# A decoder step on one core: the last block as straight code with its end by tiles and column halves, the head tokens' parts side by side, and the keys of a head turned together

## The chip, the core and the metric

The kernel runs on one core of a Trainium2 chip. The core has a matrix engine (TensorE, PE in the profile; its weight loads are shown as PEld), a vector engine (VectorE, DVE), a scalar engine (ScalarE, ACT), a general engine (GpSimd, POOL), and an engine that here issues nearly all transfers (SyncE, SP). They work from a shared on-chip memory (SBUF); TensorE writes into accumulation banks (PSUM), eight banks of 512 columns in 128 partitions. Each engine runs its own instruction list, and the lists meet at semaphores. The metric is the device time of one execution in microseconds.

## The reference

One step of a decoder trunk with one layer. 2048 prompt tokens, led by 16 meta tokens, and 8 sample sequences of 4 tokens go through the same weights (D_MODEL 1024, four recurrent heads of 128, D_FF 2816):

```python
def trunk_layer(x, pool_prev, pool_start, S0, conv_prev, lead, n1, w_in, w_pool, pool_scale, lb, g_norm,
                w_out, n2, w_a, w_b, conv_w, conv_b, w_down):
    h = rmsnorm(x, n1)
    z = h @ w_in
    y_pool, pool_new = pool_mix(z[..., :D_POOL], pool_prev, pool_start, w_pool, pool_scale)
    y_rec, S_new = hgrn2_mix(z[..., D_POOL:], S0, lb, g_norm, lead)
    x = x + jnp.concatenate([y_pool, y_rec], axis=-1) @ w_out
    y_ffn, conv_new = conv_ffn(rmsnorm(x, n2), conv_prev, w_a, w_b, conv_w, conv_b, w_down)
    return x + y_ffn, pool_new, S_new, conv_new
```

`hgrn2_mix` is a gated linear attention with a matrix state per head: in each window of tokens the output is masked scores times v, plus q (with its decay) times the state, and the state becomes its decayed self plus the window's decayed keys times v. `conv_ffn` is gelu(conv(h @ w_a)) * (h @ w_b) @ w_down with a causal convolution over three rows. A final RMSNorm gives the outputs y; the last 15 pooling inputs, the states and the last 2 rows of h @ w_a are outputs too (the histories).

## The kernel before

**Blocks.** The prompt is done in four blocks of 512 tokens (`BLOCKS`, `TILES` = 4 tiles of 128). The 16 meta and 32 sample tokens are the "head" tokens, 48 rows (`HEAD`), and go with block 0 only (`hd` = 1 in the code). Each engine's list has `body(0, 1)` as straight code and then a hardware loop, `Fori(1, BLOCKS)`, with `body(b, 0)` for blocks 1 to 3. After the loop stand the turning of the histories (L1203, L1206), their copies on ScalarE (L1667, L1671) and the last stores.

**Three products for one.** Every operand of a large product is split into a high part in fp32r and a low part, what the high part leaves. `three` (L580 to L582) makes a product of high by high, low by high and high by low, all into one bank. In block 0 the weights come raw from HBM, POOL splits them (L552 the high, L556 the low part), SP stores the split units (1 MB each, 96 of them) to HBM, and blocks 1 to 3 load them from there into four slots; a slot is loaded again when TensorE has counted its unit in `unit_done`.

**Order of a block.** The products with w_in by features (forget gates, q, u, gate) and by tokens (v); attention; W_out by tokens; residual and norm; the up products, in an inner loop; and the down products. The down products run over two column halves n, and in each over 22 units of the inner dimension (`pair`, `ktile`), for each unit over the four tiles, in block 0 also the head tokens as a fifth tile with 48 stationary columns. ScalarE casts a unit's activations to the high part (L1573), DVE makes the low part (L2274). Behind some pairs of the second half stand the norm rows of the next block, `row_transposes` (L627), whose rows `x_next` are loaded and squared during the first half. In block 3 they are computed too, from block 0's rows, and nothing uses them. After a half, DVE adds the result tile by tile to x (`half_residual`, L2197, the head tokens' piece L2199). After the second half come the squares (ScalarE, L1217), the root, and the final scaling of whole tiles (DVE, L2313); SP stores y of a block during the next block's products, and of block 3 after the loop (L503), followed by states, pooling rows and convolution rows (L529 to L533).

**Attention** runs over 16 items, four heads times four windows. For item i TensorE turns the decayed keys of the *next* item (`kd_transposed`, L830) into bank 5, ScalarE copies them to SBUF (`kd_tokens`, L1417), and `outputs` makes the masked scores by v (L842), q by the state (L846) and the keys by v (L849), which DVE adds to the state (L2137). L849 waits for the next item's copy, so that it may write its bank.

## Time and profile before

| | |
|---|---|
| runs | 2557.63, 2551.93 and 2554.62 us, median 2554.62 |
| the execution in the profile | 2552.1 us, of which the span is 2550.3 |
| mean granted clock of TensorE | 0.993 |
| TensorE | 2478.0 us busy, 13263 matmuls |
| VectorE, ScalarE, GpSimd | 1187.0, 726.6 and 407.7 us busy |
| transfers | 489.03 MB, mean 192 GB/s |

Times are microseconds from the start of the span. The end of a matmul is modelled, and matmuls overlap, so their pace is read from start to start. An instruction's row gives its start, its length, engine and line, the operation, output and input, and in brackets the idle time of the engine ahead of it with what ended it.

### The profile page before, as it was taken

How to read it: one execution, taken by the hardware profiler on the slowest of the kernel's cores; microseconds unless marked ns; L12 is line 12 of the kernel's file. 1: busy time of each engine (PE TensorE's matmuls, PEld its weight loads, DVE VectorE, ACT ScalarE, POOL GpSimd, SP SyncE). 2: the span in 40 equal slices, each digit the busy share in tenths (PEclk: the TensorE clock that was granted, in tenths of full speed). 3: DMA queues.
4: the chain of work that ended last, by engine and by line, in shares of the span. 5: the costliest groups of instructions: out<-in, count | busy, mean ns of one | idle time of the engine just before them, and what ended most of it. 6: DMA issues, size and time to landing. Idle time of an engine off the chain costs nothing.

```text
span 2550.3 us, 36515 instructions
## 1 busy us (share of the span) xinstructions
PE 2478.0 (97%) x13263; PEld 2100.9 (82%) x13263; DVE 1187.0 (47%) x2307; ACT 726.6 (28%) x1467; POOL 407.7 (16%) x311
## 2 busy tenths in 40 slices
PE   7988999999999999999999999999999999999997
PEld 7878799998778888888887888888887887888886
DVE  6777474333348754222245874222246684222234
ACT  4324132222224332111233332111233342211133
POOL 2235255555540300000000110000000020000000
PEclk9989999999999999999999999999999999999999
DMA  7732467676767224555656424555656523555653
GB/s 246 255 117 75 148 235 262 249 252 244 274 247 263 103 103 178 184 195 184 236 194 238 164 83 154 197 192 186 234 198 214 201 99 132 189 190 188 231 202 133
DMA packets 145350, 489.03 MB, mean 192 GB/s; under 512 B 8881, under 2 KB 79778, under 8 KB 96025
## 3 DMA queue, kind: packets, MB, share of 16 engines
q1 hardware_dynamic: 136747, 482.58, 52.8%
q10 hardware_dynamic: 8472, 4.75, 0.6%
q8 instruction: 77, 1.26, 0.2%
q14 instruction: 54, 0.44, 0.1%
HBM read 375.45 MB, written 112.02 MB: 191 GB/s over the span
## 4 chain that ended last, share of the span: by engine, by line
PE 91%; DVE 3%; issue 2%; DMA 2%; ACT 1%; POOL 1%; SPq 0%; DVEq 0%; ACTq 0%
PE ps L580 23%; PE ps L582 23%; PE ps L581 23%; PE ps L646 12%; PE ps L817 3%; PE ps L627 1%; PE ps L842 1%; DMA w_both<-w_split 1%; PE ps L849 1%; PE ps L611 1%; POOL w_both L556 0%; DVE arena L2115 0%; PE ps L814 0%; PE ps L906 0%; DMA w_raw<-in_w_in 0%
## 5 line engine op out<-in xcount | busy, mean ns | idle before, releaser
L580 PE MATMUL ps<-h_hi,w_both 128*128 128x512 f32 (+1 forms) x1536 | 586.6, 382 | 2.7 <-issue 2.7
L582 PE MATMUL ps<-h_lo,w_both 128*128 128x512 f32 (+1 forms) x1536 | 583.1, 380 | 0.0
L581 PE MATMUL ps<-h_hi,w_both 128*128 128x512 f32 (+1 forms) x1536 | 579.5, 377 | 0.0
L582 PEld LDWEIGHTS ps<-h_lo,w_both 128*128 128x128 f32 x1536 | 288.7, 188 | 59.7
L581 PEld LDWEIGHTS ps<-h_hi,w_both 128*128 128x128 f32 x1536 | 288.6, 188 | 58.8
L580 PEld LDWEIGHTS ps<-h_hi,w_both 128*128 128x128 f32 x1536 | 288.3, 188 | 58.3 <-issue 3.6
L580 PE MATMUL ps<-w_both,act_hi 128*128 128x512 f32 (+1 forms) x748 | 297.4, 398 | 1.8 <-DVE x_tok L2197 1.8
L582 PE MATMUL ps<-w_both,act_hi 128*128 128x512 f32 (+1 forms) x748 | 296.1, 396 | 0.0
L581 PE MATMUL ps<-w_both,act_lo 128*128 128x512 f32 (+1 forms) x748 | 295.5, 395 | 0.0
L2274 DVE TENSOR_TENSOR act_lo<-arena,act_hi 128x512 fp32r<-128x512 f32 (+1 forms) x176 | 137.5, 783 | 329.9 <-ACT act_hi L1573 329.4
L646 PE MATMUL ps<-h_hi,w_both 128*128 128x304 f32 (+1 forms) x1664 | 285.3, 294 | 2.7 <-ACT arena L1379 1.7
L389 POOL TENSOR_TENSOR arena<-arena 128x256 f32<-128x256 f32 x63 | 45.0, 715 | 1304.1 <-DVE arena L2081 1301.9
L2234 DVE SCALAR_TENSOR_TENSOR arena<-arena,vec 128x512 f32<-128x512 f32 x88 | 68.4, 777 | 396.1 <-ACT arena L1499 395.3
L646 PEld LDWEIGHTS ps<-h_hi,w_both 128*128 128x128 f32 x1664 | 237.1, 190 | 3.9 <-ACT arena L1379 2.6
L556 POOL TENSOR_TENSOR w_both<-w_raw,w_both 128x1024 fp32r<-128x1024 f32 x86 | 211.6, 2461 | 7.2
L1573 ACT CAST act_hi<-arena 128x512 fp32r<-128x512 f32 (+3 forms) x176 | 110.5, 630 | 349.2 <-PE ps L582 349.2
L646 PE MATMUL ps<-h_lo,w_both 128*128 128x304 f32 x832 | 174.8, 291 | 0.0
L580 PEld LDWEIGHTS ps<-w_both,act_hi 128*128 128x128 f32 (+1 forms) x748 | 138.3, 185 | 37.4 <-DVE x_tok L2197 2.2
L582 PEld LDWEIGHTS ps<-w_both,act_hi 128*128 128x128 f32 (+1 forms) x748 | 137.9, 184 | 36.3 <-issue 0.2
L581 PEld LDWEIGHTS ps<-w_both,act_lo 128*128 128x128 f32 (+1 forms) x748 | 138.0, 185 | 35.4 <-issue 0.2
L1498 ACT COPY arena<-ps 128x512 f32<-128x512 f32 x66 | 38.7, 586 | 447.5 <-PE ps L582 447.5
L580 PE MATMUL ps<-w_both,h_hi 128*128 128x512 f32 (+1 forms) x408 | 163.6, 401 | 2.1 <-DMA w_both<-w_split 2.1
(254 smaller groups left out, 3323.3 us busy)
## 6 DMA issues: line engine op xcount, KB each, us to landing
w_both<-w_split SPq DMA_DIRECT2D x288, 1024.0 KB, 4.8
w_split<-w_both SPq DMA_DIRECT2D x96, 1024.0 KB, 6.3
w_raw<-in_w_down SPq DMA_DIRECT2D x24, 512.0 KB, 4.3
w_raw<-in_w_a SPq DMA_DIRECT2D x22, 512.0 KB, 4.3
w_raw<-in_w_b SPq DMA_DIRECT2D x22, 512.0 KB, 4.3
w_raw<-in_w_in SPq DMA_DIRECT2D x20, 512.0 KB, 5.5
x_tok<-in_x_prompt SPq DMA_DIRECT2D x16, 512.0 KB, 6.9
arena<-in_x_prompt SPq DMA_DIRECT2D x16, 512.0 KB, 6.8
```

The source lines that it names most:

```text
L389: engine.tensor_tensor(o[:, :, 0:half], bb, gg[:, :, 0:half], ALU.subtract)
L556: nc.gpsimd.tensor_tensor(w_lo[:, s, :], w_raw[:, s, 0, :], w_hi[:, s, :].bitcast(F32), ALU.subtract).then_inc(w_ready, 1)
L580: nc.tensor.matmul(out, lhs[0], rhs[0], start=first, stop=False)
L581: nc.tensor.matmul(out, lhs[1], rhs[0], start=False, stop=False)
L582: return nc.tensor.matmul(out, lhs[0], rhs[1], start=False, stop=last)
L611: last = nc.tensor.matmul(out, w[0][:, k, :], h_lo[:, k, cols], start=False, stop=k == KD - 1)
L646: last = nc.tensor.matmul(out, lhs[:, k, :], rhs[:, k, cols], start=(k, n) == (0, 0), stop=(k, n) == (KD - 1, 2))
L817: last = nc.tensor.matmul(out, m, m, start=True, stop=True)
L1498: nc.scalar.copy(a_ext[:, r, 2:2 + BLOCK], ps[:, r, :])
L1573: nc.scalar.copy(act_hi[:, kk, lo:WIDE], acts[:, bass.ds(2 * i + kk, 1), lo:WIDE].rearrange("p a b -> p (a b)")).then_inc(act_hi_ready, 1)
L2234: own.mark(v.scalar_tensor_tensor(out=cv, in0=ae[:, 1:1 + BLOCK], scalar=w1, in1=cv, op0=ALU.mult, op1=ALU.add))
L2274: v.tensor_tensor(act_lo[:, kk, lo:WIDE], acts[:, bass.ds(2 * i + kk, 1), lo:WIDE].rearrange("p a b -> p (a b)"), act_hi[:, kk, lo:WIDE].b ...
```

## The change

Four things are changed.

1. The loop runs over blocks 1 and 2; block 3 is straight code on each engine (`first(b)` and `final(b)` tell the blocks apart).
2. In block 3 the next block's rows are not loaded, squared, normed and turned. The histories are turned in the second half of down, after pairs 2 and 6. The last two units of the second half go tile by tile (six matmuls for a tile) behind one wait for both units' low parts. The first column half of x is squared and multiplied by the final norm's vector during the second half; behind the last products, roots are taken for two tiles at a time, ScalarE scales front halves and DVE back halves, and y is stored in eight half-column stores behind the other outputs.
3. In block 0 the head tokens' low and high parts lie side by side in one operand of 112 columns (low in 0 to 47, high from 64 on). W_out and down do two matmuls in place of three for them: both by the weights' high part, both by the low part. The result lies in two row groups, which DVE adds one after the other. (The product of low by low is computed along with it.) The v products stay as they were.
4. In attention the four windows' keys of a head are turned together at the head's end, copied in two pieces, and L849 waits at a head's first window only.

```diff
+            def head_product(bank, both, w, first, last):
+                nc.tensor.matmul(ps[0:SIDE + HEAD, bank, :], both, w[0], start=first, stop=False)
+                return nc.tensor.matmul(ps[0:SIDE + HEAD, bank, :], both, w[1], start=False, stop=last)
+            def head_rows_product(bank, k, kk, w):
+                return head_product(bank, h_side[:, k, 0:SIDE + HEAD], [v[:, kk, :] for v in w], k == 0, k == KD - 1)
...
-                def kd_transposed(i):
-                    h, w, n = i // TILES, i % TILES, 16 * b + i
-                    if w == 0:
-                        pe.wait_ge(kd_ready, 4 * b + h + 1)
-                        pe.wait_ge(qe_ready, 4 * b + h + 1)
-                    if not (isinstance(n, int) and n < 1):
-                        pe.wait_ge(kdt_ready, n)
-                    if not (isinstance(n, int) and n < 2):
-                        pe.wait_ge(s_ready, n - 1)
-                    nc.tensor.transpose(ps[:, 5, 0:P], kd[:, h % 2, win(w)], ident).then_inc(kdt_done, 1)
+                def kd_transposed(h):
+                    pe.wait_ge(kd_ready, 4 * b + h + 1)
+                    pe.wait_ge(qe_ready, 4 * b + h + 1)
+                    if not (first(b) and h == 0):
+                        pe.wait_ge(s_ready, 16 * b + 4 * h)
+                    for w in range(TILES):
+                        last = nc.tensor.transpose(ps[:, 5, win(w)], kd_at(h, hd)[:, win(w)], ident)
+                    last.then_inc(kdt_done, 1)
...
-                    pe.wait_ge(kdt_ready, n + (2 if i + 1 < HEADS * TILES else 1))
-                    nc.tensor.matmul(ps[:, 5, P:2 * P], kd_tok[:, i % 2, :], v_tok[:, w, hc], start=True,
+                    if w == 0:
+                        pe.wait_ge(kdt_ready, 2 * (4 * b + h + 1))
+                    nc.tensor.matmul(ps[:, 5, 0:P], kd_token(w, hd), v_tok[:, w, hc], start=True,
                                      stop=True).then_inc(su_done, 1)
...
-                    if i + 1 < HEADS * TILES:
-                        kd_transposed(i + 1)
                     outputs(i)
...
+                    if i % TILES == TILES - 1 and i + 1 < HEADS * TILES:
+                        kd_transposed((i + 1) // TILES)
...
+            def histories(part):
+                pe.wait_ge(x2_ready, 8 * (BLOCKS - 1) + 4)
+                if part == 0:
+                    for g in range(HEADS):
+                        last = nc.tensor.transpose(ps[0:POOL_BUF, 4, win(g)], u_hist[:, g, :], ident)
+                    last.then_inc(last_t, 1)
+                else:
+                    pe.wait_ge(last_taken, 2)
+                for f in range(12 * part, min(FT, 12 * part + 12)):
+                    last = nc.tensor.transpose(ps[0:2, 5 + f % 12 // 4, win(f % 4)], conv_hist[:, f, :], ident)
+                last.then_inc(last_t, 1)
+            def last_tiles(b):
+                for kk in range(2):
+                    weights(b, U_DOWN + 22 + kk, 2 + kk, U_DOWN // 4 + 5)
+                pe.wait_ge(act_lo_ready, 2 * FT * (b + 1))
+                for t in range(TILES):
+                    for kk in range(2):
+                        last = three(ps[:, down_bank(1, t, 0), :], (act_hi[:, kk, main(t)], act_lo[:, kk, main(t)]),
+                                     [w[:, 2 + kk, kk * 512:(kk + 1) * 512] for w in (w_hi, w_lo)], False, kk == 1)
+                    last.then_inc(last_tile, 1)
...
+                    if n and final(b):
+                        for i in range(1, 10):
+                            pair(i, i % 4, False)
+                            if i in (2, 6):
+                                histories(i // 6)
+                        last_tiles(b)
+                        continue
...
-            with pe.Fori(1, BLOCKS) as b:
+            with pe.Fori(1, BLOCKS - 1) as b:
                 body(b, 0)
...
+            body(BLOCKS - 1, 0)
```

ScalarE's and DVE's sides of it:

```diff
-                def kd_tokens(i):
-                    n = 16 * b + i
-                    act.wait_ge(kdt_done, n + 1)
-                    if not (isinstance(n, int) and n < 2):
-                        act.wait_ge(su_done, n - 1)
-                    nc.scalar.copy(kd_tok[:, i % 2, :], ps[:, 5, 0:P]).then_inc(kdt_ready, 1)
+                def kd_tokens(h):
+                    act.wait_ge(kdt_done, 4 * b + h + 1)
+                    if not (first(b) and h == 0):
+                        act.wait_ge(su_done, 16 * b + 4 * h)
+                    for half in range(2):
+                        nc.scalar.copy((kd_late[1 - hd] if half else kd_tok)[:, :, :],
+                                       ps[:, 5, 2 * half * P:2 * (half + 1) * P].rearrange("p (a b) -> p a b", a=2)
+                                       ).then_inc(kdt_ready, 1)
...
+            def head_part(c, bank, side, ready=None):
+                x = x_tok[0:HEAD, TILES, c]
+                last = v.tensor_tensor(x, x, ps[side:side + HEAD, bank, :], ALU.add)
+                if side:
+                    own.mark(last)
+                else:
+                    last.then_inc(ready, 1)
...
+                if hd:
+                    head_part(c, to(TILES), SIDE)
                 for t in range(TILES):
                     v.tensor_tensor(x_tok[:, t, c], x_tok[:, t, c], ps[:, to(t), :], ALU.add).then_inc(ready, 1)
                     if hd and t == 0:
-                        v.tensor_tensor(x_tok[0:HEAD, TILES, c], x_tok[0:HEAD, TILES, c],
-                                        ps[0:HEAD, to(TILES), :], ALU.add).then_inc(hready, 1)
+                        own.settle()
+                        head_part(c, to(TILES), 0, hready)
...
+                add(0)
+                add(1)
+                variance(0)
+                add(2)
+                newton(0)
+                back(0)
+                add(3)
+                back(1)
+                variance(1)
+                newton(1)
+                back(2)
+                back(3)
```

The last twelve lines are DVE's order behind the last products: `add` adds a tile's second column half to x, `variance` and `newton` make the roots of two tiles, `back` scales a back half. ScalarE squares back halves 0 and 1, makes the first guess for tiles 0 and 1, squares half 2, scales front half 0, squares half 3, makes the second guess, and scales the other front halves.

## Rows read from the trace of the kernel before

**Rows 1.** Summary page: span, busy time of each engine, chain's shares, instruction transfers.

```profile
span 2550.3 us, 36515 instructions
...
PE 2478.0 (97%) x13263; PEld 2100.9 (82%) x13263; DVE 1187.0 (47%) x2307; ACT 726.6 (28%) x1467; POOL 407.7 (16%) x311
...
q8 instruction: 77, 1.26, 0.2%
...
PE 91%; DVE 3%; issue 2%; DMA 2%; ACT 1%; POOL 1%; SPq 0%; DVEq 0%; ACTq 0%
```

**Rows 2.** Waits of TensorE, whole run: us in total, times, longest.

```profile
PE ps L849 <- ACT arena L1417: 9.9, 14, 1.5
PE ps L830 <- DVE state L2137: 9.1, 9, 1.7
...
PE ps L580 <- issue: 2.7, 2, 1.4
```

**Rows 3.** Timeline of TensorE, two units of block 0's down products.

```profile
676.00 0.39 PE L580 MATMUL ps<-w_both,act_hi 128*48 128x512 f32 x1
...
680.19 0.39 PE L580 MATMUL ps<-w_both,act_hi 128*128 128x512 f32 x1
```

**Rows 4.** Waits of TensorE, 602 to 764 us, block 0's down products.

```profile
PE ps L580 <- DVE x_tok L2197: 1.8, 1, 1.8
```

**Rows 5.** Timeline, turn of column halves in block 0's down products.

```profile
682.87 0.67 DVE L2199 TENSOR_TENSOR x_tok<-x_tok,ps 48x512 f32<-48x512 f32 x1
...
684.19 0.50 PE L580 MATMUL ps<-w_both,act_hi 128*128 128x512 f32 x1 [1.77 <-DVE x_tok L2197]
```

**Rows 6.** Timeline of POOL: one subtraction of a weight split in block 0.

```profile
671.89 2.77 POOL L556 TENSOR_TENSOR w_both<-w_raw,w_both 128x1024 fp32r<-128x1024 f32 x1
```

**Rows 7.** Windows: length, PE, PEld, DVE, ACT, POOL, clock, DMA share, GB/s.

```profile
686.00:688.00 2.00, 2.00 (x6) 1.55 (x5) 0.98 (x3) 0.66 (x1) 1.45 (x2) 0.50 0.60 255
```

**Rows 8.** Timeline of DVE, head tokens' add of W_out in block 0.

```profile
303.59 0.68 DVE L1804 TENSOR_TENSOR x_tok<-x_tok,ps 48x512 f32<-48x512 f32 x1 [10.68 <-PE ps L582]
```

**Rows 9.** Waits of TensorE, 264 to 345 us, W_out and first up, block 0.

```profile
PE ps L605 <- POOL w_both L556: 2.2, 2, 1.9
```

**Rows 10.** Waits of TensorE, 825 to 935 us, block 1's attention.

```profile
PE ps L830 <- DVE state L2137: 1.7, 1, 1.7
PE ps L849 <- ACT arena L1417: 1.2, 3, 0.9
PE ps L830 <- ACT arena L1417: 0.4, 1, 0.4
```

**Rows 11.** Timeline of block 1's attention, the longest wait for a key copy.

```profile
906.06 0.27 ACT L1417 COPY arena<-ps 128x128 f32<-128x128 f32 x1
...
906.37 0.49 PE L849 MATMUL ps<-arena 128*128 128x128 f32 x2 [0.92 <-ACT arena L1417]
```

**Rows 12.** Waits of TensorE, 165 to 262 us, block 0's attention.

```profile
PE ps L849 <- ACT arena L1417: 6.2, 5, 1.5
```

**Rows 13.** Timeline of block 3's down, one group of the unused norm's transposes.

```profile
2502.61 1.03 PE L627 MATMUL ps<-tab,arena 128*128 128x128 f32 x8
...
2503.72 0.39 PE L581 MATMUL ps<-w_both,act_lo 128*128 128x512 f32 x1
```

**Rows 14.** Timeline of block 3's down, start of the last two units.

```profile
2526.67 0.39 PE L580 MATMUL ps<-w_both,act_hi 128*128 128x512 f32 x1
...
2527.76 0.69 DVE L2274 TENSOR_TENSOR act_lo<-arena,act_hi 128x512 fp32r<-128x512 f32 x1 [2.13 <-ACT act_hi L1573]
```

**Rows 15.** Timeline behind the last matmul.

```profile
2532.47 2.48 DVE L2197 TENSOR_TENSOR x_tok<-x_tok,ps 128x512 f32<-128x512 f32 x4 [4.01 <-PE ps L582]
...
2536.86 1.06 ACT L1217 ACTIVATE arena<-x_tok 128x1024 f32<-128x1024 f32 x1
...
2539.52 4.87 DVE L2313 SCALAR_TENSOR_TENSOR x_tok<-x_tok,norms,arena 128x1024 f32<-128x1024 f32 x4
```

**Rows 16.** Windows, stores of y at the end, columns as in rows 7.

```profile
2542.00:2546.00 4.00, 0.00 (x0) 0.00 (x0) 2.40 (x3) 0.41 (x2) 0.00 (x0) 0.50 1.01 408
```

More of the change, by code:

```diff
@@ L112, in shape_tables, with first, final @@
     return t
+def first(b):
+    return isinstance(b, int) and b == 0
+def final(b):
+    return isinstance(b, int) and b == BLOCKS - 1
 class Order:
@@ L454, in body @@
                     unit(b, s, U_Q + s, U_Q // 4, raw(s, KD), w_in_t[:, :, 512 + s * P:512 + (s + 1) * P])
-                if not isinstance(b, int):
+                if not first(b):
                     store_y(b - 1)
@@ L488, in body @@
                                 sp.wait_ge(act_ready, FT * (b + 1))
-                            for t in range(TILES):
+                            for t in () if final(b) else range(TILES):
                                 sp.dma_start(x_next[:, t, :],
@@ L559, in ahead @@
             def ahead(b):
-                for h in (1, 2, 3) if isinstance(b, int) else (2, 3):
+                for h in (1, 2, 3) if first(b) else (2, 3):
                     if h == 1:
@@ L571, in _ @@
                 units(j)
-            with pool.Fori(1, BLOCKS) as b:
+            with pool.Fori(1, BLOCKS - 1) as b:
                 ahead(b)
+            ahead(BLOCKS - 1)
         @block.tensor
@@ L1128, in ktile @@
                                 pe.wait_ge(x2_ready, 8 * b + 2)
-                            cols = main(t) if t < TILES else slice(0, HEAD)
-                            out = ps[:, down_bank(n, t, hd), :] if t < TILES else ps[0:HEAD, down_bank(n, t, hd), :]
-                            last = three(out, (act_hi[:, kk, cols], act_lo[:, kk, cols]),
-                                         [w[:, slot, wk * 512:(wk + 1) * 512] for w in (w_hi, w_lo)], first, fin)
+                            ws = [w[:, slot, wk * 512:(wk + 1) * 512] for w in (w_hi, w_lo)]
+                            if t == TILES:
+                                last = head_product(down_bank(n, t, hd), act_wide[:, kk, 0:SIDE + HEAD], ws, first, fin)
+                                continue
+                            last = three(ps[:, down_bank(n, t, hd), :], (act_hi[:, kk, main(t)], act_lo[:, kk, main(t)]),
+                                         ws, first, fin)
                         return last
@@ L1255, in decays @@
                         g = g_t[:, h, HEAD:WIDE]
-                        if not (isinstance(b, int) and h == 0):
+                        if not (first(b) and h == 0):
                             act.wait_ge(s_ready, 16 * b if h < 2 else 16 * b + 4 * (h - 1))
@@ L1606, in body @@
                 pair(1, 0, True)
+                if final(b):
+                    last_columns(b, pair)
+                    return
                 root_guess(var[:, :], rstd[:, :], var_ready, 2 * b + 2, guess_ready)
@@ L1663, in _ @@
             body(0, 1)
-            with own.loop(1, BLOCKS, 14) as b:
+            with own.loop(1, BLOCKS - 1, 14) as b:
                 body(b, 0)
-            act.wait_ge(last_t, 1)
-            nc.scalar.copy(last_rows[0:POOL_BUF, :], ps[0:POOL_BUF, 0, :]).then_inc(last_taken, 1)
-            act.wait_ge(last_t, 2)
-            for i in range(6):
-                m = min(4, FT - 4 * i) * P
-                last = nc.scalar.copy(conv_rows[0:2, 4 * i * P:4 * i * P + m], ps[0:2, 1 + i, 0:m])
-            last.then_inc(last_taken, 1)
+            body(BLOCKS - 1, 0)
             act.wait_ge(u_rows_ready, 17)
@@ L2089, in operand @@
                     dve.wait_ge(su_done if i else a_done, n)
+                if first(b) and h and i == LEVELS:
+                    dve.wait_ge(kdt_done, h)
                 dve.wait_ge(dec_exp, 8 * (4 * b + h) + i + 1)
@@ L2285, in down @@
                     pair(0, i)
+                if final(b):
+                    last_columns(b, pair)
+                    return
                 dve.wait_ge(squared, 12 * b + 12)
@@ L2353, in _ @@
             body(0, 1)
-            with own.loop(1, BLOCKS, 122) as b:
+            with own.loop(1, BLOCKS - 1, 122) as b:
                 body(b, 0)
+            body(BLOCKS - 1, 0)
 def kernel(x_prompt, x_sample, state_pool, state_rec, state_conv, meta_tokens, norm1_g, w_in, w_pool, pool_scale,
```

208 lines of the change are left out of this document (159 added, 49 removed).

## The prediction

> **What bounds the kernel now.** I read the summary page first. TensorE is busy for 97% of the span and holds 91% of the chain that ended last; DVE, the next engine, is busy for 47% [rows 1]. So a matmul that disappears is worth its full pitch, and work of another engine counts only where TensorE waits for it or after TensorE's last matmul. Second, the waits of TensorE over the whole run, to see how much idle time there is to win: the large rows are the attention's, 9.9 us for ScalarE's copy of the turned keys (L1417) and 9.1 us for DVE's state (L2137), and 2.7 us are the two returns of the hardware loop [rows 2]. Third, the timelines of the places that the diff touches. The run profiled took 2552.1 us against a span of 2550.3; the sum below is made against 2552.1. The median of the three runs, 2554.62, lies 2.5 above it.
>
> **Head tokens side by side.** In block 0's down products each head product is three matmuls with 48 stationary columns, and they leave at the same pitch as the wide ones: 4.19 us for the 18 starts from 676.00 to 680.19 (three with 48 columns, twelve with 128, three with 48 again), which is 0.233 each [rows 3]. A pitch of the wide matmuls that differed from the narrow ones' would show in that count of 18, so for 112 columns I take 0.233 too. So a product falls from three to two, 0.233 saved. Down has 22 units of the inner dimension times two column halves, 44 products: 10.25 us. W_out has 8 times two, 16 products: 3.73 us. The V products keep three.
>
> What this adds: the result lies in two row groups of a bank, so DVE adds two 48x512 pieces where it added one. At the turn from the first column half of down to the second, TensorE has its only wait of that stage, 1.77 us for DVE's second tile [rows 4, 5]; DVE does a 128x512 and a 48x512 add ahead of it, the latter 0.67 us [rows 5]. The extra add and its settle come ahead of that second tile, so the wait grows by 0.67 to 0.9; I take 0.9. Down: -9.35. It has a cover to lose: block 0's weights are split by POOL, and the subtraction begun at 671.89 took 2.77 us, to 674.66, for a product that starts at 680.19, a lead of 5.5 us [rows 3, 6]. TensorE's unit gets about 0.47 us shorter (two products), so over the three units until POOL's slot is reused the lead falls by about 1.4; 4 us stay. Without that lead the saving would be bounded by POOL.
>
> After the 1.77 us wait the granted clock stands at 0.50 in 686 to 688, the lower level of 1.2 GHz [rows 7]. The wait does not vanish, so I leave that cost (about 1.5 us, an estimate: eight matmuls at some 0.43 instead of 0.23) where it is.
>
> In W_out the saving passes through two other chains: DVE's head add, 0.68 us, now twice [rows 8], and POOL's split of the next weights, for which TensorE waits 2.2 us right behind this stage already [rows 9]. Those splits start when TensorE frees a slot, which comes earlier too, so most of the gain gets through. Bounds: -3.73 (all of it) to 0 (POOL's chain sets the time). I take -3.3, as the slot's release moves with the products. Head tokens: -9.35 - 3.3 = -12.65.
>
> **Keys of a head together.** In block 1 the waits of the attention are 1.7 us on the state, 1.2 on ScalarE's key copies in three places and 0.4 more on them ahead of the transposes, whose bank the copy frees [rows 10]. The largest, 0.92 us at 906.37, is a copy of 0.27 us that started only at 906.06 [rows 11]. With one transposition and two copies for a head, thirteen of sixteen items need nothing from ScalarE: 1.2 + 0.4 = 1.6 us go, and some 0.2 at about four restarts (the row at 906.37 shows 0.49 us for two where a running pair has 0.39), 0.9 together: -2.5. Against it, at three head boundaries two copies of 256 columns must both end before the first key product: from the 0.27 us of 128 columns [rows 11] an estimated 0.4 each, so 0.8 in place of 0.27, of which about 0.2 lies behind outputs that are issued first: +0.35 each, +1.05. I take -1.5 for each of blocks 1 to 3, -4.5; bounds -2.5 (the copies hidden) and +1.5 (the copies late behind ScalarE's other work at each head). The 1.7 us on the state stay: the product with the state waits for the same event if the transpose no longer does.
>
> In block 0 the same copies cost 6.2 us in five waits [rows 12], because ScalarE's exponentials stand ahead of them. Half of it I expect to move to the next thing late (DVE's masking and POOL's exponents of the head): -3.1, with +0.4 for the extra pieces in the pool rows of the head: -2.7, bounds -6 and +1.
>
> **Straight last block.** One of two loop returns goes: 2.7/2 [rows 2], -1.4. The four groups of eight transposes of the unused norm go: from the first of them at 2502.61 to the second matmul behind them at 2503.72 are 1.11 us, less one pitch of 0.23: 0.88 a group [rows 13], 3.5 together. The 26 history transposes that move in from behind the loop cost 0.11 each, by the same row, 2.9, and 0.1 of restarts: +3.0. Net -0.5. They stand where the outputs of the first half have long been added.
>
> **Last two units tile by tile.** The first tile now waits for the low parts of both units. Before, the product began at 2526.67 while DVE's low part of the second unit started at 2527.76 (0.69 us, to 2528.45) [rows 14]. TensorE can start at about 2528.5: +1.9, bounds 1.7 and 3.6, the upper if the clock falls behind it as in [rows 7]. ScalarE and DVE have nothing else queued there that is longer than that, if their front-half work is done by then.
>
> **The end.** DVE starts the last adds at 2532.47, right behind the last matmul's end E, and the span ends at 2550.3, 17.9 us later [rows 1, 15]. In between stand four adds (2.48 us, 0.62 each), four squares of 1024 columns of which the last starts at 2536.86 (1.06 us), the root, and four scalings of 1.22 us from 2539.52 on [rows 15]; the stores follow. After: the tiles come 1.4 us apart (six matmuls of 0.233), so that three of them are added, squared or stored before E. Behind E stand one add (0.62), one half square (1.06/2 and its read, 0.7), the root (1.6, from 2537.92 to 2539.52) and two half scalings (1.2): 4.1 us, and I add 2 for the hand-overs between engines and ScalarE's front halves, an estimate: E+6.1. Six of the eight stores of 256 KB are then left, from E+5.7 on at the 408 GB/s of 2542 to 2546 [rows 16], 0.64 us each: to E+9.6. With 0.8 to close the span, an estimate, it is E+10.4. So 17.9 - 10.4: -7.5; bounds -5 (hand-overs of 4 us) and -9 (none, and the stores at the root's heels).
>
> **Sum.** -12.65 - 2.7 - 4.5 - 1.4 - 0.5 + 1.9 - 7.5 = -27.35: 2552.1 - 27.35 = 2524.75. I say 2525. Own range 2518 to 2531.
>
> **Rivals.** (1) Grouping the keys pays nothing: ScalarE's two copies are late at every head and each boundary gives back what the items save. For it: the 906.06 copy was late behind ScalarE's own work [rows 11], and that work stays. Against: only three boundaries a block are left. 2525 + 4.5 + 2.7 = 2532.
>
> (2) Block 0's down becomes bound by weights: POOL was 2.77 us on half a unit [rows 6], and if a unit's chain of load, split and store is not released by TensorE but runs at its own rate, the 9.35 are lost: 2534. Against it: no wait on POOL is among the waits of down in block 0 [rows 4].
>
> (3) The other side: the straight block pays for its code. Instruction transfers are 77 packets of 1.26 MB in all, 16 KB each [rows 1]. TensorE's straight code of one block is an estimated 18 such packets (about 3,300 matmuls a block by a quarter of 13263, less those in the up loop, two instructions each). If each were waited for like a loop return, 1.35 us, that is +24, and 2549, or 2552 with some on the other engines. Slower by over 0.2% needs 27.35 + 5.1 = 32.45 us, 24 such waits. Against it: block 0 is straight code already, and its waits on issue are only the loop's two [rows 2].
>
> The Trainium skill (Runtime: NRT & Kernel Launch, "Instruction fetch mechanics") says that sequential code is streamed ahead mostly hidden and that a taken branch out of the window forces a fetch before execution goes on. By that rule rival 3 costs nothing and the -1.4 stands; the two 1.3 us gaps at the returns agree.
>
> (4) More is won: the keys' grouping reaches its bounds (-2.5 a block and -6): 2525 - 3.0 - 3.3 = 2518.7, and with an end of -9, 2517.
>
> **Chances.** The forecast 0.5; rival 1 0.2; rival 2 0.07; rival 4 0.15; rival 3 0.08, of which half ends slower. The bound of a readable difference is 0.2%, 5.1 us. Faster 0.92, same 0.04, slower 0.04. The range reaches from rival 4 with a little more from its end (2513) to rival 2 with a low gain at the end (2538).
>
> **What would show it.** Right: L581 on the 128*48 operands gone from down, two instructions with 112 columns at a pitch of 0.23; the 1.77 us wait at the column turn grown to some 2.6; no wait of the key products on ScalarE except at a head's first item; one loop return; an idle of about 1.9 us before the last tiles; and 10.4 us from the last matmul to the end of the span. Wrong: a pitch above 0.23 at 112 columns, issue waits spread over block 3, waits on POOL in block 0's down, or the half-tile stores ending later than E+9.6.

## The result and the profile after

The changed kernel took 2533.69 us (median of 4 runs, 2528.01 to 2536.31) against 2553.27 before: ratio 0.9914, interval 0.9901 to 0.9928, so 19.6 us less. In two later sets of runs the same code stood 25.0 us (ratio 0.9902, 0.9888 to 0.9917) and 23.8 us (0.9909, 0.9892 to 0.9925) below the kernel before. The forecast was 2525 with a range of 2513 to 2538: the direction, the range and most of the terms held, and the gain that was forecast, 27.35 us, was 2 to 8 us too large. The narrower "own range" of 2518 to 2531 holds the two later medians, 2529.80 and 2529.40, and not the first. The number alone would fit rival 1 (2532) and rival 2 (2534) as well; only the stages tell them from the forecast.

The summary page of the changed kernel, to be read against [rows 1]:

```profile
span 2526.2 us, 35716 instructions
...
PE 2460.3 (97%) x13171; PEld 2097.3 (83%) x13171; DVE 1178.4 (47%) x2346; ACT 717.1 (28%) x1435; POOL 409.5 (16%) x311
...
q8 instruction: 74, 1.21, 0.2%
...
PE 91%; DVE 3%; DMA 2%; ACT 1%; issue 1%; POOL 1%; SPq 0%; DVEq 0%; ACTq 0%
```

The span is 24.1 us shorter and TensorE is as full as before. The straight code did not cost more instruction transfers: 74 packets against 77.

Where the 24.1 us lie is read from the starts of the first and the last matmul of each stage in the two traces (a scores product starts attention, and its end is taken as the start of the last window's scores; a product with the activations starts down). "Again" is a second trace of the same code.

| stage | before | changed | difference | again | forecast |
|---|---|---|---|---|---|
| start to the end of block 0's attention | 250.44 | 248.99 | -1.5 | -1.6 | -2.7 |
| block 0, from there to down | 350.89 | 347.51 | -3.4 | -3.0 | -3.3 |
| block 0, down | 162.27 | 155.92 | -6.35 | -6.6 | -9.35 |
| block 1, down's end before it to its down | 462.18 | 460.65 | -1.5 | -1.5 | -1.5 |
| block 2, the same | 463.92 | 462.51 | -1.4 | +0.2 | -1.5 |
| block 3, the same, with the loop's return | 463.97 | 460.74 | -3.2 | -3.3 | -2.9 |
| block 3, down | 126.12 | 127.32 | +1.2 | +1.2 | +1.4 |
| last matmul's start to the end | 18.28 | 10.35 | -7.9 | -7.9 | -7.5 |

(In block 2 of the second trace the granted clock falls to 0.50 for 3.4 us from 1443 us on.) Two rows miss by more than 1 us: block 0's down, and the first, in which two effects of opposite sign are added up (see "The changed kernel again").

The head products in block 0's down, from the timeline of TensorE: start, length, instruction.

```profile
670.74 0.39 PE L613 MATMUL ps<-w_both,act_wide 128*128 128x512 f32 x1
...
670.97 0.39 PE L695 MATMUL ps<-w_both,act_wide 128*112 128x512 f32 x1
...
671.20 0.40 PE L696 MATMUL ps<-w_both,act_wide 128*112 128x512 f32 x1
...
671.44 0.40 PE L611 MATMUL ps<-w_both,act_wide 128*128 128x512 f32 x1
```

Two in place of three [rows 3], 0.23 to 0.24 apart: 112 columns leave at the pitch of 128, as assumed. So the 10.25 us were saved, and something gave part of them back. The waits of TensorE from 596 to 770 us, block 0's down, where before there was one of 1.8 us [rows 4]:

```profile
PE ps L611 <- DVE x_tok L2342: 3.0, 1, 3.0
PE ps L611 <- DVE act_lo L2419: 1.6, 2, 1.1
```

The wait at the turn of the column halves grew by 1.2 us (forecast 0.9), and there are new ones of 1.6 us for DVE's low parts: -10.25 + 1.2 + 1.6 = -7.45, where -6.35 was measured. Of the 1.1 between them some 0.4 are, by an estimate, restarts behind the waits; 0.7 I can't assign.

Attention of block 0, the waits from 165 to 262 us, against [rows 12]:

```profile
PE ps L884 <- DVE arena L2260: 6.5, 5, 2.7
...
PE ps L893 <- ACT arena L1539: 1.5, 1, 1.5
```

The 6.2 us in five waits for ScalarE's key copies are one wait of 1.5, and 6.5 us in five places now go to DVE's last step on the masked scores (L2260): part of the stall went to the next thing late. Part of it is gone: with the waits of attention that are not shown here (4.2 us on DVE's state before, none now) its waits were 12.3 us in 14 places and are 10.1 in 7. In block 1 (820 to 935 us, against [rows 10]) no key copy is waited for:

```profile
PE ps L871 <- DVE state L2276: 1.9, 2, 1.8
PE ps L770 <- DVE arena L2305: 0.5, 1, 0.5
PE ps L884 <- DVE arena L2265: 0.3, 1, 0.3
```

The last units and the end, from the timeline, against [rows 14, 15]:

```profile
2508.49 0.40 PE L613 MATMUL ps<-w_both,act_wide 128*128 128x512 f32 x1
...
2510.41 0.47 PE L611 MATMUL ps<-w_both,act_wide 128*128 128x512 f32 x1 [1.52 <-DVE act_lo L2419]
...
2515.87 0.40 PE L613 MATMUL ps<-w_both,act_wide 128*128 128x512 f32 x1
...
2520.42 1.41 DVE L2495 SCALAR_TENSOR_TENSOR x_tok<-x_tok,norms,arena 128x512 f32<-128x512 f32 x2
...
2522.67 0.64 SPq L563 DMA_DIRECT2D out_y_prompt<-x_tok  x1
```

TensorE stands 1.5 us before the last tiles. With E for the end of the last matmul, 2516.27, the back halves are scaled by 2521.8, which is E+5.6 where the forecast had E+6.1, and the span ends at E+9.9 (forecast E+10.4).

### The profile page after: what moved, and what is told of

Its sections match the earlier page's. It is cut to its first block, busy times and chain, and to the rows that moved or that the text cites. A ratio compares the mean times of both kernels' runs of the same rounds, so it can differ in the third digit from the quotient of the medians.

```text
span 2526.2 us, 35716 instructions
## 1 busy us (share of the span) xinstructions
PE 2460.3 (97%) x13171; PEld 2097.3 (83%) x13171; DVE 1178.4 (47%) x2346; ACT 717.1 (28%) x1435; POOL 409.5 (16%) x311
## 4 chain that ended last, share of the span: by engine, by line
PE 91%; DVE 3%; DMA 2%; ACT 1%; issue 1%; POOL 1%; SPq 0%; DVEq 0%; ACTq 0%
PE ps L611 23%; PE ps L613 23%; PE ps L612 23%; PE ps L677 13%; PE ps L861 3%; PE ps L884 1%; PE ps L658 1%; DVE arena L2254 1%; PE ps L642 1%; DMA w_both<-w_split 1%; PE ps L695 1%; PE ps L696 1%; PE ps L893 1%; POOL w_both L586 0%; PE ps L950 0%
## 5 line engine op out<-in xcount | busy, mean ns | idle before, releaser
L611 PE MATMUL ps<-w_both,act_wide 128*128 128x512 f32 x704 | 280.7, 399 | 6.1 <-DVE act_lo L2419 3.1
L613 PE MATMUL ps<-w_both,act_wide 128*128 128x512 f32 x704 | 278.6, 396 | 0.0
L612 PE MATMUL ps<-w_both,act_lo 128*128 128x512 f32 x704 | 278.2, 395 | 0.0
L2419 DVE TENSOR_TENSOR act_lo<-arena,act_wide 128x512 fp32r<-128x512 f32 x176 | 122.8, 699 | 244.3 <-ACT act_wide L1696 244.1
L1696 ACT CAST act_wide<-arena 128x512 fp32r<-128x512 f32 (+3 forms) x176 | 110.5, 630 | 349.8 <-PE ps L613 249.2
L611 PEld LDWEIGHTS ps<-w_both,act_wide 128*128 128x128 f32 x704 | 132.9, 189 | 39.0 <-DVE x_tok L2342 3.4
L611 PE MATMUL ps<-w_both,h_hi 128*128 128x512 f32 (+1 forms) x392 | 157.4, 401 | 2.1 <-DMA w_both<-w_split 2.1
L613 PEld LDWEIGHTS ps<-w_both,act_wide 128*128 128x128 f32 x704 | 132.6, 188 | 32.0
L612 PEld LDWEIGHTS ps<-w_both,act_lo 128*128 128x128 f32 x704 | 132.8, 189 | 30.4
```

What stands on the lines that cost most here:

```text
L611: nc.tensor.matmul(out, lhs[0], rhs[0], start=first, stop=False)
L612: nc.tensor.matmul(out, lhs[1], rhs[0], start=False, stop=False)
L613: return nc.tensor.matmul(out, lhs[0], rhs[1], start=False, stop=last)
L1696: nc.scalar.copy(act_hi[:, kk, lo:WIDE], acts[:, bass.ds(2 * i + kk, 1), lo:WIDE].rearrange("p a b -> p (a b)")).then_inc(act_hi_ready, 1)
L2419: last = v.tensor_tensor(out[:, kk, cols], acts[:, bass.ds(2 * i + kk, 1), cols].rearrange("p a b -> p (a b)"), act_hi[:, kk, cols].bitcas ...
```

## Experiments

**Each part alone.** Three kernels take over one part of the change each: the head tokens' parts (4 of its lines below), the keys, and the last block.

```diff
+act_wide = sb("act_wide", [P, 2, SIDE + WIDE], F32R)
+h_side = ...  # [P, KD, 2 * SIDE]
+last = head_product(down_bank(n, t, hd), act_wide[:, kk, 0:SIDE + HEAD], ws, first, fin)
+head_part(c, to(TILES), SIDE); own.settle(); head_part(c, to(TILES), 0, hready)
```

> The kernel before with the head tokens' parts side by side and nothing else of the change. First theory (each part keeps its own effect, and the parts add): block 0's W_out 3.4 us shorter, its down products 6.3 us shorter, with the wait at the turn of the column halves near 3 us instead of 1.77 and one or two waits of 0.5 to 1.2 us for the low part made by DVE; in all 9 to 10 us below the kernel before. Second theory (the down products lost their 3 us to something of the other parts, as the memory that the keys and the last block use): the down products 9 to 10 us shorter here, in all 12 to 13 us. On the stage of the sample tokens ahead of attention, which was 4 us longer in the changed kernel's profile: if that is a clock that varies from execution to execution, it may fall here or not, and does not follow the edit; if the changed kernel's code makes it, one of the three part kernels must show it and the others not.

Measured: 2547.06 against 2554.46, -7.4 us (0.997, 0.9958 to 0.9982). In its trace W_out to down is 2.75 us shorter and down 3.95, with a wait of 3.8 at the turn and 1.8 for low parts: the shortfall belongs to this part and the other parts don't make it. The second theory fell. The first was too high, by about 2 us in all; in down, 6.9 us stood at a granted clock of 0.50 here and 3.4 in the kernel before's trace.

```diff
-for i: kd_transposed(i + 1); outputs(i)
+for i: outputs(i); ...; if i % TILES == TILES - 1: kd_transposed((i + 1) // TILES)
```

> The kernel before with the keys of a head turned and copied together, and nothing else. First theory: blocks 1 to 3 each 1.5 us shorter in attention, as in the changed kernel; block 0's attention 3 to 6 us shorter, part of which hangs on the granted clock there; in all 7.5 to 10 us below the kernel before. Second theory (grouping pays nothing by itself; what attention gained came from the clock at its start): blocks 1 to 3 within 0.3 us of before each, and block 0 within 1 us when compared at the same clock; in all 0 to 2 us.

Measured: 2547.75, -6.7 us (0.9971, 0.9962 to 0.998), less than the 7.5 to 10 of the first theory. In its trace block 0's attention is 81.0 us long where it was 85.7, so 4.6 shorter, with 5.5 us of it at a granted clock of 0.50 in place of 8.2. Block 3 is 1.6 us shorter from down to down; blocks 1 and 2 were not shorter in this trace, and the windows of the three blocks' attention at the same place show why (columns as in [rows 7]):

```profile
866.00:868.00 2.00, 2.00 (x6) 1.71 (x7) 1.93 (x5) 0.58 (x3) 0.00 (x0) 0.50 0.00 0
...
1457.00:1459.00 2.00, 2.00 (x7) 1.52 (x6) 2.00 (x5) 0.00 (x0) 0.58 (x1) 0.50 0.00 0
2045.00:2047.00 2.00, 1.93 (x15) 1.66 (x14) 1.93 (x3) 1.32 (x5) 0.00 (x0) 1.00 0.00 0
```

In blocks 1 and 2 the granted clock fell to 0.50, the level of 1.2 GHz, for 3.4 us right behind the wait of 1.8 us on DVE's state, and in block 3, behind the same wait, it did not. One such fall costs about the 1.5 us that a block wins. Grouping pays; the second theory fell.

```diff
-with pe.Fori(1, BLOCKS) as b: body(b, 0)
+with pe.Fori(1, BLOCKS - 1) as b: body(b, 0)
+body(BLOCKS - 1, 0)   # with histories, last_tiles and last_columns
```

> The kernel before with block 3 as straight code and its new end, and nothing else. First theory: one return of the loop less (1.6 us), the down products of block 3 1.2 us longer (1.7 us idle ahead of the last two units against 0.5 us fewer transposes), 10.2 to 10.4 us from the last matmul to the end of the span instead of 17.9: in all 8 to 8.5 us below the kernel before. Second theory (straight code pays at its pages, and the other parts hide it): waits on issue spread over block 3, and in all less than 5 us.

Measured: 2543.42, -11.0 us (0.996, 0.9947 to 0.9974; the -8 to -8.5 of the first theory is inside). In the trace: loop's return -1.7, down +1.2, end 10.37 us from the last matmul's start, one wait on issue of 1.4 in the whole run. The stages named give -8.4; the rest of the -11.0 I can't assign, though its five runs had mean clocks of 0.992 to 0.994, where most of the 16 runs beside them had 0.990 to 0.992. The three parts sum to -7.4 - 6.7 - 11.0 = -25.1; the whole change gave -25.0 and -23.8 in the later sets. The parts add within their intervals, each of which is 2 to 3.5 us wide to either side; that they meet to a tenth is luck.

**The changed kernel again**, unaltered.

> The changed kernel once more, unaltered, as the measure for the other three on one chip. First theory (between the profile of before, 2552.1, and that of the changed kernel, 2528.0, lies 27 us of work less 4 us of clock, and the clock is drawn anew in each execution): the stage of the sample tokens, from 100 to 182 us, again has two to four falls of the granted clock to 0.5 for 6.8 us or longer, at other places than in the first profile; the stages behind it as in the first profile within 0.4 us where the clock stands at 1.00; median 19 to 25 us below the kernel before. Second theory (the changed code itself fixes the falls): the same falls at the same places, and the start of attention again at 168.9.

Measured: 2529.80 against 2554.84. The clock fell at other places than in the first profile, so the second theory fell. TensorE reached block 0's attention at 165.10 us here and at 168.91 in the first trace, since the clock fell more often in the sample tokens' stage there; attention's last scores product started at 248.88 and 248.99. So attention itself was 3.7 us longer here. Its window in three traces, the kernel with the head part alone, the changed kernel and "again" (columns as in [rows 7], the clock is the third number from the end):

```profile
168.89:252.84 83.95, 72.27 (x574) 69.38 (x573) 64.88 (x96) 34.35 (x101) 44.97 (x49) 0.98 0.18 64
...
168.91:248.99 80.08, 70.61 (x574) 69.06 (x574) 64.38 (x94) 33.62 (x93) 44.96 (x49) 0.98 0.19 67
...
165.10:248.88 83.78, 74.32 (x574) 72.82 (x574) 64.56 (x94) 33.60 (x93) 44.96 (x49) 0.93 0.18 64
```

| trace | keys | attention starts | its length | of it at 0.50 | length less half of that |
|---|---|---|---|---|---|
| before | one by one | 164.76 | 85.68 | 8.2 | 81.6 |
| head part alone | one by one | 168.89 | 83.95 | 3.8 | 82.1 |
| keys alone | of a head together | 170.89 | 81.04 | 5.5 | 78.3 |
| changed | of a head together | 168.91 | 80.08 | 3.8 | 78.2 |
| again | of a head together | 165.10 | 83.78 | 11.7 | 77.9 |
| last two units in another order (below) | of a head together | 170.15 | 83.33 | 11.0 | 77.8 |

The waits of attention are the same in the changed kernel and in "again" (6.5 us in five places on L2260 in both), so these don't absorb a late start: the stage is as long as its work and its waits, plus half of the time that the clock stands at 0.50. The last column, an estimate on that footing, is 77.8 to 78.3 us in nine traces with the keys together and 81.5 to 82.1 in the four with single keys. The two traces that start within 0.02 us of each other at a mean clock of 0.98, the head part alone and the changed kernel, differ by 3.9 us. So in block 0 the keys gave 3.3 to 3.9 us. Between the profiles of before and changed, attention starts 4.15 us later, with the clock at 0.50 for 23.5 us ahead of it in place of 12.3, and its own clock gives 2.2 us back; this net loss of 2.0 us hid part of the keys' gain in the table's first row, -1.5. The first theory's clock, 4 us in its estimate, was there, and half of it came back inside attention. (In block 0's down, too, the near agreement of the table, -6.35 and -6.6, has two parts: "again" waits 2.8 us for low parts where the first trace waits 1.6, and its clock does not fall there.)

Whether the change itself makes the clock fall more often ahead of attention stays open. Attention starts at 164.4 to 167.2 us in the three traces without the head part and the keys (before, the last block alone, and the one with two subtractions below) and at 165.1 to 170.9 in ten that have one of them or both, so the head part alone (168.89) and the keys alone (170.89) both show the later start, which the expectation for the head part wanted of one part only. The mean clocks of whole runs don't decide it: they are 0.9915 in the 47 runs of the kernel before that stand beside the experiments and 0.9916 in the 12 of the changed kernel, but they count the end, where TensorE is idle and the clock stands at 0.50 for 12 us in the profile of before and for 5 to 7 in those of the changed kernel.

**The order of the last two units.**

```diff
-for t in range(TILES): for kk in range(2): ...          # behind one wait for both low parts
+for t, kk in ((0,0), (1,0), (0,1), (1,1), (2,0), (2,1), (3,0), (3,1)): ...   # a wait for each kk
```

> The changed kernel with the last two units in another order: the first unit's products for tiles 0 and 1, then the second unit's for both, then tiles 2 and 3 with both units each; only the second unit's products wait for its low part. First theory (the 1.7 us idle ahead of the last tiles is the wait for the second unit's low part, and 1.4 us of products fit into it): the idle falls to 0.3 us or less, tile 0 is ready 0.7 us later against the last matmul and nothing waits for it there, since the root of tiles 0 and 1 waits for tile 1: 1.3 to 1.5 us shorter than the changed kernel. Second theory (something behind the last matmul sets the end, as the stores or ScalarE's chain): the end moves back with the idle by less than 0.5 us.

Measured: 2529.05 against 2554.46 (0.9904, 0.9891 to 0.9918). No wait stands in block 3's down from 2400 us on; the stage is 125.89 us where the changed kernel's is 127.32 (-1.4), and the end is 10.51 where it was 10.35. In the trace the first theory held; no runs of the changed kernel stand in the same set, so the times don't show it.

**The order of DVE's adds at the turn.**

```diff
-head rows 64 to 111; tile 0; head rows 0 to 47; tile 1; tile 2; tile 3
+tile 0; tile 1; head rows 64 to 111; tile 2; head rows 0 to 47; tile 3
```

(The rows from 64 on are the high part's and are added first; the expectation has the two names the other way round.)

> The changed kernel with another order of DVE's adds at the two ends of block 0's down halves: tiles 0 and 1 first, then the head tokens' low part, tile 2, the head tokens' high part, tile 3. First theory (the wait of 2.97 us at the turn is DVE's queue, two adds of the head tokens ahead of tile 1, of which the change brought one): the wait falls by 1.3 us to 1.6 or 1.7; where the clock no longer falls behind it, 1.6 us more are won; median 1 to 3 us below the changed kernel. Second theory (the wait is for DVE's low part, late behind POOL, and not for the adds): the wait falls by less than 0.5 us.

Measured: 2528.45 against 2529.80 for the changed kernel, not to be told apart. The waits of its down in block 0:

```profile
PE ps L611 <- DVE act_lo L2420: 4.2, 4, 2.5
PE ps L611 <- DVE x_tok L2346: 1.5, 1, 1.5
```

The turn's wait fell from 3.0 to 1.5, as the first theory has it, and in this execution the waits for low parts grew to 4.2 us, so that down took 157.71, with one fall of the clock as in the changed kernel. The largest of them in the timeline, with the engine after the length:

```profile
679.48 0.22 DVE L2420 TENSOR_TENSOR act_wide<-arena,act_wide 128x64 fp32r<-128x64 f32 x1
679.52 2.40 POOL L586 TENSOR_TENSOR w_both<-w_raw,w_both 128x1024 fp32r<-128x1024 f32 x1
...
679.63 2.84 DVE L2420 TENSOR_TENSOR act_lo<-arena,act_wide 128x512 fp32r<-128x512 f32 x1
...
682.61 0.47 PE L611 MATMUL ps<-w_both,act_wide 128*128 128x512 f32 x1 [2.45 <-DVE act_lo L2420]
```

DVE's 128x512 subtraction took 2.84 us, where the changed kernel's 176 of them take 0.70 on average; it began 0.1 us behind POOL's subtraction and ended 0.6 behind its end. The kernel before has the same delay, and its trace could have shown it ahead of the prediction:

```profile
620.89 2.40 POOL L556 TENSOR_TENSOR w_both<-w_raw,w_both 128x1024 fp32r<-128x1024 f32 x1
620.96 2.93 DVE L2274 TENSOR_TENSOR act_lo<-arena,act_hi 128x560 fp32r<-128x560 f32 x1 [3.48 <-ACT act_hi L1573]
```

There 18 of the 44 subtractions of block 0's down took over 1 us, all of them while POOL worked, and TensorE waited for none [rows 4]. The nine that met no work of POOL took 0.74 us at most.

**What makes the waits for low parts.** The changed part brings DVE a second instruction for each unit, and it makes TensorE's unit shorter. Two kernels take these apart. The first has both new orders, of the last units and of DVE's adds, and the shorter unit without the instruction (from the third unit on the head tokens' new low part is left out):

```diff
-((act_wide, slice(0, SIDE)), (act_lo, slice(HEAD, WIDE)))[1 - hd:]
+((act_wide, ...), (act_lo, ...))[0 if hd and n == 0 and isinstance(i, int) else 1:]
```

> The kernel with both new orders, without DVE's 128x64 subtraction in block 0's down products except for the first two units (so the head tokens are multiplied with a stale low part from the third unit on; the number and form of the matmuls stays). First theory (the new waits of 0.4 to 2.5 us for DVE's low parts come from the second subtraction that the side-by-side operand needs): those waits vanish from 600 to 765 us, or one of under 0.5 us stays, and the down products are 1.5 to 2 us shorter than with both orders. Second theory (they come from TensorE itself, whose unit is 0.47 us shorter, so that a subtraction that is held up while POOL's runs is no longer covered): the waits stay at two or three, 1.2 us or more together.

Measured: 2525.80 against 2552.20 (0.9903, 0.9879 to 0.9927). Its waits in block 0's down:

```profile
PE ps L611 <- DVE act_lo L2420: 3.0, 2, 2.3
PE ps L611 <- DVE x_tok L2346: 1.3, 1, 1.3
```

The second has the instruction in the kernel before:

```diff
-v.tensor_tensor(act_lo[:, kk, 0:WIDE], ...)
+v.tensor_tensor(act_lo[:, kk, 0:64], ...); v.tensor_tensor(act_lo[:, kk, 64:WIDE], ...)
```

> The kernel before with DVE's 128x560 subtraction of block 0's down products cut into a 128x64 and a 128x496 one, and nothing else: the extra instruction with TensorE's old pace. First theory (the second subtraction makes the waits): two or three waits for the low part of 0.4 to 2 us in the down products, 1 to 3 us slower there. Second theory (TensorE's shorter unit makes them): no wait for the low part, the stage within 0.3 us of before at the same clock.

Measured: 2554.84 against 2552.20 (1.0011, 1.0 to 1.0022). Its waits there:

```profile
PE ps L580 <- DVE x_tok L2197: 2.8, 1, 2.8
PE ps L580 <- DVE act_lo L2275: 0.3, 1, 0.3
```

Without the instruction the waits for low parts stay (3.0 us), and with it at the old pace they don't come (0.3; the kernel with the keys alone, at the old pace without it, shows one of 0.4). The first theory fell, and the second holds for the waits: TensorE's shorter unit no longer covers a subtraction that is held up beside POOL's. Its other half, a stage within 0.3 us, did not: down took 163.84 us against 162.27, of which 1.0 is the wait at the turn (2.8 against 1.8 [rows 4]). DVE's last two subtractions ahead of it took 2.25 us, beside POOL's, where the single one took 1.26; how much of this is the extra instruction and how much the moment at which POOL worked, one trace does not show.

**Both orders together.**

> The changed kernel with both new orders, of DVE's adds at the turn and of the last two units' products. First theory: the two gains add, 2.5 to 4 us below the changed kernel in the stages (1.3 at the turn, 1.4 ahead of the last tiles), which the medians of five runs show only roughly, since the clock moves single runs by 3 us either way. Second theory: one of the two is taken back at the end by the stores: less than 1.5 us.

Measured: 2529.61 against 2529.80, with single runs from 2524.09 to 2532.61: not decided. So both were run once more side by side.

> The kernel with both new orders again, beside the changed kernel on one chip, because the clock moved single runs by more than the 2.8 us that the stages show (1.3 to 1.5 at the turn, 1.5 ahead of the last tiles). First theory: its median lies 2 to 4 us below the changed kernel's. Second theory (the waits that the turn frees come back as waits for DVE's low parts, as the kernel with the turn alone showed): 0 to 1.5 us.

> The changed kernel again, unaltered, as the measure for the kernel with both orders on one chip: 24 to 26 us below the kernel before by either theory, with two to four falls of the granted clock in the stage of the sample tokens.

Measured: 2525.74 (2523.11 to 2526.86; 0.989, 0.9874 to 0.9907) against 2529.40 (2529.17 to 2532.34) for the changed kernel: -3.7 us, and no run of the one reaches the other's. In the traces block 0's down is 153.88 us against 156.01 and block 3's 125.92 against 127.34: 2.1 + 1.4. Not all of it is the orders': in block 0's down the changed kernel's trace has a fall of the clock of 3.4 us behind the turn and the other has none, which is 1.7 of the 2.1 by an estimate (half of the time at 0.50), and the mean clocks of the four runs are 0.992 to 0.994 against 0.991 to 0.993. Whether the shorter wait at the turn keeps the clock up is not shown: with the new order it fell in block 0's down in one trace of five, with the old one in two of four (three of the changed kernel, and the one with the last two units in another order). What the traces show free of the clock is 0.4 + 1.4. This is the fastest complete version of the study, 27.5 us below the kernel before in its set.

**Small products spread.** In the sample tokens' stage, each feature product cut in two around the small ones:

```diff
-feature_tile(0, U_U + h + 1, (6, 7))
+feature_half(U_U + h + 1, 0)        # and feature_half(..., 1) ahead of the outer products
```

> The kernel with both new orders, and each of the four feature products in the stage of the sample tokens (48 matmuls, 6.2 us at full clock) cut in two: the second half stands between the state products with four columns and the outer products, where the small products stood in one stretch of 5 us. First theory (the clock falls behind 5 us in which TensorE does nothing but small products, and each fall costs 3 us or more): fewer falls between 100 and 182 us, attention starts at 158 to 163 us in place of 164.8 to 170.9, the mean clock rises by 0.002 or more, and the median lies 4 to 9 us below the kernel with both orders alone. Second theory (the falls follow the share of small work over the whole stage and not its order): as many falls, and the median within 2 us.

Measured: 2538.20 against 2529.61 for both orders, 8.6 us slower. The clock still fell, and DVE became late in the stage. Waits from 120 to 190 us:

```profile
PE ps L994 <- DVE arena L2196: 5.6, 2, 3.0
PE ps L1053 <- DVE arena L2213: 2.4, 1, 2.4
```

Attention started at 179.7 us. Neither theory held. The edit moved the small products behind half a feature product more, on which, as I read the edit, DVE's next step waits, and what it would do to the clock alone it does not tell.

## Why the prediction held, and where it did not

- **Head products, two for three:** right. The pitch at 112 columns is that of 128.
- **Block 0's down, -9.35:** the step that failed; -6.35 and -6.6 were measured. I looked for the cover that could go, named POOL's splits with 5.5 us of lead, and found it ample; no wait on POOL came. But the work that lost its cover was DVE's low part, which I did not price at all: 0.7 us by itself, up to 2.84 while POOL subtracts. The kernel before, with up to 2.93, hid it behind a longer unit. The term at the turn was put at 0.9 and came out at 1.2. About 1 us of the miss stays open.
- **W_out, -3.3:** right in kind and somewhat too large. The two traces give -3.4 and -3.0, but against the longest of the old traces; by the medians of four traces with the old W_out (350.04) and nine with the new (347.59) it is -2.4.
- **Keys, -1.5 a block in blocks 1 to 3:** right where the clock stood (-1.5, -1.4, -1.6). That is what the sum took; the granted clock can take one block's gain away.
- **Keys in block 0, -2.7:** right in kind and somewhat too small: 3.3 to 3.9 us at the same clock. I expected half of the key copies' waits to move to DVE's masking; more than that did, but the waits on the state, 4.2 us, went as well. The table's -1.5 is this gain less 2.0 us of clock, for which the forecast had no term.
- **Loop, norm and last units:** right: -1.7 for -1.4, and +1.2 for +1.4 in down. The stall was 1.5 us.
- **The end, -7.5:** right (-7.9).
- **Rivals:** 1 (grouping pays nothing) and 3 (code) were refuted by the traces. Of 2 (down's gain is lost to weights) a third came about, by DVE and not by its mechanism. Waits on issue are one of 1.5 us, the loop's, in the changed kernel; the straight block shows none. The Trainium skill (Runtime: NRT & Kernel Launch, "Instruction fetch mechanics") has sequential code streamed ahead mostly hidden, and the trace agrees.
- **The base:** I summed against one profiled execution, 2552.1, whose own runs have a median of 2554.6. That the forecast was then set at 2525, and not at the 2527 that the median would give, is 2 us of the miss.

So of the forecast's 27.35 us the stages of the first trace gave 24.1. Missing are 3.0 in down and 2.0 to the clock ahead of and in block 0's attention; against them stand 0.7 more for the keys there and about 1 elsewhere. That the total came so near is partly luck, as these misses go both ways. The first set's median stood at -19.6 and the later ones at -25.0 and -23.8; by their intervals, 18 to 25, 21 to 29 and 19 to 28 us, chance is enough for that. What made the three runs at a mean clock of 0.991 in the first set slower than those of the later sets I can't say.

## What to carry over

When TensorE's time in a loop gets shorter, price again every instruction that feeds that loop at its longest duration in the trace, and not at its mean: work that was covered can become the next bound without having changed, as DVE's low part did. Order an engine's queue at a turn by what releases the bound engine, and put work that nobody waits for behind it (here the wait fell from 3.0 to 1.5 us). A gain of 1 to 2 us a stage needs traces, stage by stage, since one fall of the clock is as large; and a stage's length is to be compared at the same granted clock, not only its end against another trace's end.

## What was not expected of the hardware

DVE's subtraction of one on-chip operand from another is held while POOL runs a subtraction of its own: 2.84 us instead of 0.70 with 128x512, and a 128x64 one took 0.22 us at 679.48 in the rows above and 2.40 at 708.61 in the changed kernel's trace, with POOL's from 708.23 to 710.93. In the changed kernel's block 0 the 24 subtractions of 128x512 that met no work of POOL took 0.70 us at most, and so did the 132 of the later blocks, none of which met any. DVE's adds with one operand in PSUM are not held: 0.67 us at 675.34 and two in 1.27 at 675.93, beside POOL's subtraction from 674.97 to 677.34. The Trainium skill (GPSIMD Engine Reference, "1. Specifications") says that the two engines share their SBUF interfaces and that DVE instructions with two SBUF inputs contend; the traces agree, with these numbers.

The granted clock falls to 0.50 in stages where TensorE is nearly always busy. The sample tokens' stage of the changed kernel, TensorE busy 9.4 to 10.0 of 10 us (columns as in [rows 7]):

```profile
120.00:130.00 10.00, 9.44 (x53) 8.56 (x52) 8.87 (x35) 1.96 (x9) 3.41 (x2) 0.66 0.51 180
130.00:140.00 10.00, 9.83 (x58) 7.73 (x57) 6.47 (x24) 1.73 (x9) 3.40 (x2) 0.76 0.59 202
140.00:150.00 10.00, 10.00 (x65) 9.13 (x65) 8.44 (x39) 0.64 (x2) 0.00 (x0) 0.84 0.54 158
```

Each of the three falls there begins inside a stretch of small products (16 with four columns, outer products with 48 rows, transposes of 48). The same code had the clock at 1.00, 0.66 and 1.00 in these three windows in its second trace. Behind waits of the same length it falls in one block and not in another, as the three blocks above show. What decides it stays open here.
